# Seven block products in place of eight for the gate and up projections of a two-layer fp32 decoder

## Chip, cores and metric

The kernel runs on one core of a Trainium2 chip, as one launch. The metric is device time in microseconds (us) from start to end of the execution. Below, PE is the matrix engine (TensorE), PEld its weight loads, DVE is VectorE, ACT is ScalarE, POOL is GpSimd and SP is SyncE.

## What is computed

The input x is 512 tokens by 1024 channels in float32. Two layers run one after the other:

```python
for l in range(2):
    h = rms_norm(x, g_mix[l])
    z = h @ w_in[l]                       # 1024 x 10752
    # three mixers (retention, spatial gating, dilated attention) and gates from z
    x = x + merged @ w_o[l]
    h = rms_norm(x, g_ffn[l])
    gate, up = jnp.split(h @ w_gate_up[l], 2, axis=-1)    # 1024 x (2 x 2816)
    x = x + (jax.nn.silu(gate) * up) @ w_down[l]          # 2816 x 1024
```

The change concerns the line with gate and up. All arithmetic is float32 with float32 results.

## The kernel before

**Tiles and slabs.** Activations are held transposed: channels in partitions, the 512 tokens along the row. A layer is a list of tiles (`tiles_of_layer`, line 58). A tile is one output of 128 channels by 512 tokens, made in one PSUM bank from 4, 8 or 11 blocks of 128 x 128 weights. The feed forward is made in two halves of `FF_HALF` = 11 pairs: for each pair a tile `fgate` and a tile `fup` of 8 blocks, then 8 `down` tiles of 11 blocks that add the half to x. Tiles alternate between two main banks, so a tile can start once the tile two before it has been evacuated (`main`, in the tensor block).

**Three matmuls a block.** Full float32 precision is made from the faster float32r format. Every weight and every input is held as a high and a low part, and a block is three matmuls into the same bank: high x high, high x low, low x high (line 663). The moving operand is stored in two halves and read by turns from one and the other (`in_turn`).

**The way of a weight.** Eight blocks of 128 x 128 make a slab of 512 KB. SP loads slabs (line 551) into three raw slots; ACT copies a slab to its high part (`split`, line 829) once the slab three before it has been used; DVE subtracts to get the low part (line 994), which also frees the raw slot for SP's next load.

**The way of an output.** DVE evacuates a tile. A gate tile is multiplied by `norm_rstd` (line 1077), as h_high and h_low hold x times the gain only, and ACT applies silu (line 886). An up tile is multiplied by `norm_rstd` (line 1106) and by the gate (line 1107); ACT makes the high part (line 940) and DVE the low part (line 1128) of the product for the down tiles. A down tile is added onto x (line 1099).

**Order.** `schedule()` writes one list of steps by hand: for every tile its matmuls (`main`), the splits of the slab three ahead, what goes before the evacuation (`pre`), the evacuation (`evac`) and what follows (`post`). Each engine walks this list and does its own part in that order; semaphores tie them together. So every engine's queue is strict: a step that waits holds up all that stands behind it. SP runs a loop over slabs of its own, in which it also loads tables, and writes and reads back a small table of softmax maxima and sums per head (lines 590 to 600), which DVE needs at line 1198 (step `weigh`). GpSimd does nothing.

## Time and profile before

| | |
|---|---|
| median of 3 runs | 1954.92 us (1954.76 to 1955.07) |
| the profiled execution | 1955.0 us |
| its span, first to last instruction | 1953.2 us |
| PE busy | 1934.8 us, 99% |
| PE weight loads busy | 1690.0 us, 87% |
| DVE busy | 1135.9 us, 58% |
| ACT busy | 776.7 us, 40% |
| moved by DMA | 191.67 MB, 98 GB/s |

Busy time is the sum of the spans in which an engine had an instruction in work. Matmuls are pipelined: one is listed with its whole latency, and the next starts before it ends, so the busy time of PE says that it never stood still, and the distance between the starts says how fast it went. The granted clock of PE was 1.0 of full speed over the span. Section 5 of the page groups instructions by line and form; its last columns are the idle time just ahead of them and who ended it.

### The profile page before, as it was taken

How to read it: one execution, taken by the hardware profiler on the slowest of the kernel's cores; microseconds unless marked ns; L12 is line 12 of the kernel's file. 1: busy time of each engine (PE TensorE's matmuls, PEld its weight loads, DVE VectorE, ACT ScalarE, POOL GpSimd, SP SyncE). 2: the span in 40 equal slices, each digit the busy share in tenths (PEclk: the TensorE clock that was granted, in tenths of full speed). 3: DMA queues.
4: the chain of work that ended last, by engine and by line, in shares of the span. 5: the costliest groups of instructions: out<-in, count | busy, mean ns of one | idle time of the engine just before them, and what ended most of it. 6: DMA issues, size and time to landing. Idle time of an engine off the chain costs nothing. (4 is left out here: it accounts for less than half of the span.)

```text
span 1953.2 us, 23528 instructions
## 1 busy us (share of the span) xinstructions
PE 1934.8 (99%) x9368; PEld 1690.0 (87%) x9368; DVE 1135.9 (58%) x1523; ACT 776.7 (40%) x1090; POOL 0.2 (0%) x4
## 2 busy tenths in 40 slices
PE   7999999999999999999999999999999999999999
PEld 6888888888888888888888888888888888888888
DVE  6666667746666554355476666676366664534545
ACT  5544444533334432233345444344343343322334
POOL 0000000000000000000000000000000000000000
PEclk9999999999999999999999999999999999999999
DMA  5222222233233233333232222222223332333333
GB/s 193 87 77 76 87 82 81 92 98 98 96 120 107 97 99 98 106 107 99 97 98 92 66 79 84 82 88 94 100 97 107 109 108 97 97 97 108 98 103 123
DMA packets 65436, 191.67 MB, mean 98 GB/s; under 512 B 17200, under 2 KB 17456, under 8 KB 65328
## 3 DMA queue, kind: packets, MB, share of 16 engines
q1 hardware_dynamic: 65328, 190.17, 30.2%
q8 instruction: 75, 1.23, 0.3%
q14 instruction: 33, 0.27, 0.0%
HBM read 187.98 MB, written 2.16 MB: 97 GB/s over the span
## 5 line engine op out<-in xcount | busy, mean ns | idle before, releaser
L663 PE MATMUL bank<-h_high,w_high 128*128 128x512 f32 x2048 | 787.9, 385 | 12.3 <-DVE h_low L999 10.7
L663 PE MATMUL bank<-h_high,w_low 128*128 128x512 f32 x2048 | 777.0, 379 | 0.0
L663 PE MATMUL bank<-h_low,w_high 128*128 128x512 f32 x2048 | 776.9, 379 | 0.0
L829 ACT ACTIVATE w_high<-raw 128x1024 fp32r<-128x1024 f32 x342 | 360.9, 1056 | 951.8 <-PE bank L663 941.1
L994 DVE TENSOR_TENSOR w_low<-raw,w_high 128x1024 fp32r<-128x1024 f32 x342 | 417.1, 1222 | 91.3 <-ACT w_high L829 77.7
L663 PEld LDWEIGHTS bank<-h_high,w_high 128*128 128x128 f32 x2048 | 387.8, 189 | 70.4 <-issue 8.3
L663 PEld LDWEIGHTS bank<-h_high,w_low 128*128 128x128 f32 x2048 | 387.5, 189 | 55.1
L663 PEld LDWEIGHTS bank<-h_low,w_high 128*128 128x128 f32 x2048 | 387.9, 189 | 53.6
L663 PE MATMUL bank<-in_high,w_high 128*128 128x512 f32 x672 | 254.9, 379 | 0.0
L663 PE MATMUL bank<-in_low,w_high 128*128 128x512 f32 x672 | 254.7, 379 | 0.0
L663 PE MATMUL bank<-in_high,w_low 128*128 128x512 f32 x672 | 254.7, 379 | 0.0
L1077 DVE TENSOR_TENSOR scaled<-bank,norm_rstd 128x512 f32<-128x512 f32 x164 | 118.7, 724 | 172.9 <-PE bank L663 172.2
L663 PEld LDWEIGHTS bank<-in_high,w_high 128*128 128x128 f32 x672 | 127.0, 189 | 18.2 <-DVE in_low L1128 0.4
L663 PEld LDWEIGHTS bank<-in_high,w_low 128*128 128x128 f32 x672 | 127.0, 189 | 18.1
L663 PEld LDWEIGHTS bank<-in_low,w_high 128*128 128x128 f32 x672 | 127.0, 189 | 17.9
L1099 DVE TENSOR_TENSOR xT<-bank,xT 128x512 f32<-128x512 f32 x48 | 33.2, 692 | 147.7 <-PE bank L663 147.7
L1106 DVE TENSOR_TENSOR tmp<-bank,norm_rstd 128x512 f32<-128x512 f32 x44 | 30.4, 692 | 119.3 <-PE bank L663 117.8
L940 ACT ACTIVATE in_high<-prod 128x512 fp32r<-128x512 f32 x76 | 67.9, 894 | 78.6 <-DVEq L1096 27.5
L663 PE MATMUL bank<-work 128*128 128x128 f32 (+2 forms) x496 | 78.3, 305 | 0.0
L1128 DVE TENSOR_TENSOR in_low<-prod,in_high 128x512 fp32r<-128x512 f32 x76 | 63.4, 834 | 23.5 <-ACT in_high L940 23.5
L663 PEld LDWEIGHTS bank<-work 128*128 128x128 f32 x496 | 65.9, 191 | 6.2 <-issue 3.8
L886 ACT ACTIVATE work<-scaled 128x512 f32<-128x512 f32 x108 | 67.0, 620 | 6.4 <-DVE scaled L1077 6.2
(106 smaller groups left out, 1070.4 us busy)
## 6 DMA issues: line engine op xcount, KB each, us to landing
raw<-weights SPq DMA_DIRECT2D x343, 512.0 KB, 3.5
row<-rows SPq DMA_DIRECT2D x3, 768.0 KB, 4.5
xT<-x_t SPq DMA_DIRECT2D x8, 256.0 KB, 5.7
decay_sb<-decay SPq DMA_DIRECT2D x8, 256.0 KB, 3.8
out_t<-xT SPq DMA_DIRECT2D x8, 256.0 KB, 6.5
sgw<-spatial SPq DMA_DIRECT2D x3, 256.0 KB, 2.6
rot<-rotation SPq DMA_DIRECT2D x1, 512.0 KB, 7.8
pairs_by_token<-pairs SPq DMA_DIRECT2D x16, 4.0 KB, 4.9
```

Of the source, the lines that this page charges most:

```text
L663: return pe.matmul(o, w, m, start=start, stop=stop)
L829: act.activation(w_high[:, PART_SLOT[s], :, :], raw[:, s % RAW_SLOTS, :, :], ACT.Copy).then_inc(part_high_w.sem, 1)
L886: act.activation(dst, src, func).then_inc(activated.sem, 1)
L940: act.activation(halves(parts(key)[0]), parted(src), ACT.Copy).then_inc(high_ready.sem, 1)
L994: dve.tensor_tensor(w_low[:, PART_SLOT[s], :, :], raw[:, s % RAW_SLOTS, :, :], w_high[:, PART_SLOT[s], :, :], ALU.subtract).then_inc(part_ ...
L1077: dve.tensor_tensor(*operands, ALU.mult).then_inc(tile_stored.sem, 1)
L1099: dve.tensor_tensor(xT[:, t[-1], :], src, xT[:, t[-1], :], ALU.add).then_inc(tile_stored.sem, 1)
L1106: chain(dve.tensor_tensor(tmp[:, :], src, norm_rstd[:, :], ALU.mult))
L1128: dve.tensor_tensor(halves(lo), parted(src), halves(hi), ALU.subtract).then_inc(low_ready.sem, 1)
```

## The change

Of the 44 gate and up tiles of a layer, 8 stay as they are (`PLAIN_PAIRS` = 2, that is 4 gate and 4 up tiles). The other 36 are made in 9 units. A unit is two gate tiles and two up tiles. The inner dimension of 1024 is cut in two, and so are the 512 tokens, and the outputs are the gate and the up part: a 2 x 2 by 2 x 2 block product, A times B. It is made with seven products of quarters in place of eight (`QUICK`). Each product is 4 blocks of the inner dimension by 2 blocks of output channels by 256 tokens, three matmuls each: 24 matmuls of 256 columns. Two of the products are accumulated onto the bank of another (`ONTO`); the rest of the sums of results are made on DVE from banks and kept copies, three banks are copied or activated by ACT (`BY_SCALAR`).

The products need sums of quarters of the input (s1 to s4) and of the weights (t1 to t4). For the input, DVE first makes `normed`, x times gain times `norm_rstd` with the tokens reordered, then the sums, and ACT and DVE split the seven inputs in high and low parts, all among the steps of the eight plain tiles. The sums of weights are made in HBM before they are needed: GpSimd issues, for each unit, four plain copies and four adding transfers of 512 KB each from HBM to HBM, in six steps with a wait after each, and SP waits for them ahead of its load of a slab of sums. The down tiles are now in parts of 12 and 10 blocks; the results of a unit, f1 and f2 (each two channels tiles by 256 tokens), are stored side by side, so that the down tiles read them by turns. The load of `sgw` and `row` for the next layer moves from the first projection of branch 1 to the second down part, since the memory of `row` now also holds an input part.

```diff
+FF_BLOCKS = (12, 10)
+PLAIN_PAIRS = 2
+PAIRS = D_FF // P // 2
+QUICK_UNITS = range(PLAIN_PAIRS, PAIRS)
...
     for half in range(2):
-        for j in range(FF_HALF):
-            t += [("fgate", half, j), ("fup", half, j)]
+        if half == 0:
+            for j in range(2 * PLAIN_PAIRS):
+                t += [("fgate", 0, j), ("fup", 0, j)]
+        for u in QUICK_UNITS:
+            if (2 * u >= FF_BLOCKS[0]) == (half == 1):
+                t += [("quick", u, step) for step in range(7)]
         t += [("down", half, n) for n in range(KT)]
...
+QUICK = (("a11", "b11"), ("s2", "t2"), ("a12", "b21"), ("s1", "t1"), ("s3", "t3"), ("s4", "b22"), ("a22", "t4"))
+A11B11, S2T2, A12B21, S1T1, S3T3, S4B22, A22T4 = range(7)
+ONTO = {A12B21: A11B11, S4B22: S1T1}
+BY_SCALAR = (A11B11, A12B21, S1T1)
+SUMS = ("t1", "t2", "t3", "t4")
...
-    for half in range(2):
-        for j in range(FF_HALF):
-            post[AT["fup", half, j]] += [("high", "f", half, j), ("low", "f", half, j)]
-
+    for j in range(2 * PLAIN_PAIRS):
+        post[AT["fup", 0, j]] += [("high", "f", 0, j), ("low", "f", 0, j)]
+    for u in QUICK_UNITS:
+        post[AT["quick", u, S4B22]] += [("high", "f1", u), ("low", "f1", u)]
+        post[AT["quick", u, A22T4]] += [("second", u), ("high", "f2", u), ("low", "f2", u)]
+    post[AT["fup", 0, 0]] += [("normed", n) for n in range(4)]
+    post[AT["fgate", 0, 1]] += [("normed", n) for n in range(4, KT)]
+    post[AT["fup", 0, 1]] += [("part_high", "a11"), ("part_low", "a11"), ("input_sum", "s1")]
+    post[AT["fgate", 0, 2]] += [("input_sum", "s2"), ("part_high", "s2"), ("part_low", "s2")]
+    post[AT["fup", 0, 2]] += [("part_high", "s1"), ("part_low", "s1"), ("input_sum", "s3")]
+    post[AT["fgate", 0, 3]] += [("part_high", "s3"), ("part_low", "s3"), ("input_sum", "s4"), ("part_high", "s4"),
+                                ("part_low", "s4")]
+    post[AT["fup", 0, 3]] = [("part_high", "a12"), ("part_low", "a12")] + post[AT["fup", 0, 3]]
+    post[AT["quick", PLAIN_PAIRS, A11B11]] += [("part_high", "a22"), ("part_low", "a22")]
...
+        @block.gpsimd
+        def _(pool):
+            started = [0]
+
+            def sum_weights(dst, src, add):
+                if add:
+                    pool.dma_start(dst, src, accum_op=ALU.add, max_dma_last_dim=8 * P * 4).then_inc(weights_summed, 16)
+                else:
+                    pool.dma_start(dst, src).then_inc(weights_summed, 16)
+                started[0] += 1
+
+            for layer in range(DEPTH):
+                for n, u in enumerate(QUICK_UNITS):
+                    first = AT["quick", u, 0]
+                    b11, b21, b22 = (weights[layer * HOST_ROWS + SOURCE[BLOCKS[first + step][0][0]]]
+                                     for step in (A11B11, A12B21, S4B22))
+                    b12 = weights[layer * HOST_ROWS + B12_ROW[u]]
+                    t1, t2, t3, t4 = (sums_dram[layer, n, w] for w in range(4))
+                    sum_weights(t1, b11, False)
+                    sum_weights(t3, b22, False)
+                    pool.wait_ge(weights_summed, 16 * started[0])
+                    sum_weights(t1, b12, True)
+                    sum_weights(t3, b12, True)
+                    pool.wait_ge(weights_summed, 16 * started[0])
+                    sum_weights(t2, t1, False)
+                    pool.wait_ge(weights_summed, 16 * started[0])
+                    sum_weights(t2, b22, True)
+                    pool.wait_ge(weights_summed, 16 * started[0])
+                    sum_weights(t4, t2, False)
+                    pool.wait_ge(weights_summed, 16 * started[0])
+                    sum_weights(t4, b21, True)
+                    pool.wait_ge(weights_summed, 16 * started[0])
...
+            def load(layer, s):
+                slot, source = s % RAW_SLOTS, SOURCE[s]
+                if isinstance(source, tuple):
+                    n = source[0] - PLAIN_PAIRS
+                    sp.wait_ge(weights_summed, 16 * 8 * (layer * len(QUICK_UNITS) + n + 1))
+                    source = sums_dram[layer, n, SUMS.index(source[1])]
+                else:
+                    source = weights[layer * HOST_ROWS + source]
+                sp.dma_start(raw[:, slot, :, :].rearrange("p a n -> p (a n)"), source).then_inc(
...
-                    if s == behind(("proj", 1, 0)):
-
-                        sp.wait_ge(score_taken.sem, score_taken.at(base, "mix", HEADS - 1))
+                    if s == behind(("down", 1, 0)):
+
+                        sp.wait_ge(tile_done.sem, tile_done.at(base, AT["quick", PAIRS - 1, A22T4]))
...
+            def quick(base, i, o):
+
+                _, u, step = TILES[i]
+                slot = PART_SLOT[BLOCKS[i][0][0]]
+                high, low = input_parts(QUICK[step][0])
+                if u == PLAIN_PAIRS:
+                    pe.wait_ge(part_low.sem, part_low.at(base, QUICK[step][0]))
+                pe.wait_ge(part_low_w.sem, part_low_w.at(base, BLOCKS[i][0][0]))
+                for k in range(4):
+                    hi, lo = in_turn(high[:, k, :]), in_turn(low[:, k, :])
+                    for c in range(2):
+                        part = o[:, c * 2 * P:(c + 1) * 2 * P]
+                        wh, wl = w_high[:, slot, 2 * k + c, :], w_low[:, slot, 2 * k + c, :]
+                        onto = step in ONTO
+                        pe.matmul(part, wh, hi, start=k + c == 0 and not onto, stop=False, skip_group_check=onto)
+                        pe.matmul(part, wh, lo, start=False, stop=False, skip_group_check=onto)
+                        last = pe.matmul(part, wl, hi, start=False, stop=k == 3 and c == 1, skip_group_check=onto)
+                last.then_inc(tile_done.sem, 1)
...
+                            if t[2] in BY_SCALAR:
+                                act.wait_ge(tile_done.sem, tile_done.at(base, i))
+                            if t[2] == A11B11:
+                                if t[1] > PLAIN_PAIRS:
+                                    act.wait_ge(tile_stored.sem, tile_stored.at(base, AT["quick", t[1] - 1, S2T2]))
+                                act.activation(kept_first, bank_of(base, i)[:, :], ACT.Copy).then_inc(bank_copied.sem, 1)
+                            elif t[2] == A12B21:
+                                if t[1] > PLAIN_PAIRS:
+                                    act.wait_ge(product.sem, product.at(base, "f1", t[1] - 1))
+                                else:
+                                    act.wait_ge(product.sem, product.at(base, "f", 0, 2 * PLAIN_PAIRS - 1))
+                                act.activation(first_gate, bank_of(base, i)[:, :], ACT.Silu).then_inc(bank_copied.sem, 1)
+                            elif t[2] == S1T1:
+                                if t[1] > PLAIN_PAIRS:
+                                    act.wait_ge(product.sem, product.at(base, "f2", t[1] - 1))
+                                act.activation(kept_s1t1, bank_of(base, i)[:, :], ACT.Copy).then_inc(bank_copied.sem, 1)
+                            elif t[2] == A22T4:
+                                act.wait_ge(tile_stored.sem, tile_stored.at(base, i))
+                                act.activation(sum3, sum3, ACT.Silu).then_inc(second_gate.sem, 1)
...
+                            first = i - t[2]
+                            if t[2] == S2T2:
+                                dve.wait_ge(bank_copied.sem, bank_copied.at(base, first + A11B11))
+                                dve.tensor_tensor(sum2, src, kept_first, ALU.add).then_inc(tile_stored.sem, 1)
+                            elif t[2] == S3T3:
+                                dve.wait_ge(tile_stored.sem, tile_stored.at(base, first + S2T2))
+                                dve.tensor_tensor(sum3, src, sum2, ALU.add).then_inc(tile_stored.sem, 1)
+                                dve.wait_ge(bank_copied.sem, bank_copied.at(base, first + S1T1))
+                                dve.wait_ge(tile_stored.sem, tile_stored.at(base, i))
+                                chain(dve.tensor_tensor(kept_s1t1, kept_s1t1, sum3, ALU.subtract))
+                            elif t[2] == S4B22:
+                                tmp_free()
+                                dve.tensor_tensor(tmp[:, :], src, sum2, ALU.subtract).then_inc(tile_stored.sem, 1)
+                                dve.wait_ge(tile_stored.sem, tile_stored.at(base, i))
+                                dve.wait_ge(bank_copied.sem, bank_copied.at(base, first + A12B21))
+                                dst = product_slot(("f1", t[1]))
+                                tmp_read.append((product, ("f1", t[1])))
+                                dve.tensor_tensor(dst, first_gate, tmp[:, :], ALU.mult).then_inc(product.sem, 1)
+                            else:
+                                dve.tensor_tensor(sum3, src, sum3, ALU.add).then_inc(tile_stored.sem, 1)
...
+                    elif kind == "second":
+                        u, = key
+                        dve.wait_ge(second_gate.sem, second_gate.at(base, u))
+                        dst = product_slot(("f2", u))
+                        dve.tensor_tensor(dst, sum3, kept_s1t1, ALU.mult).then_inc(product.sem, 1)
+                    elif kind == "normed":
+                        n, = key
+                        dve.scalar_tensor_tensor(normed[:, n, :, :], xT[:, n, :].rearrange("p (q m) -> p m q", m=4),
+                                                 vec[:, n:n + 1], norm_rstd[:, :].rearrange("p (q m) -> p m q", m=4),
+                                                 ALU.mult, ALU.mult).then_inc(normed_ready.sem, 1)
```

The lines left out hold the same pattern: the sums of the input and their parts, the signals, the layout of the weights on the host, and the placement of the new buffers over old ones that rest in the feed forward.

## Rows read from the trace of the kernel before

**Rows 1.** Page: busy time, share of the span, instructions; slices of PE and clock.

```profile
PE 1934.8 (99%) x9368; PEld 1690.0 (87%) x9368; DVE 1135.9 (58%) x1523; ACT 776.7 (40%) x1090; POOL 0.2 (0%) x4
...
PE   7999999999999999999999999999999999999999
...
PEclk9999999999999999999999999999999999999999
```

**Rows 2.** PE timeline, plain tile: start us, us, engine, line, operation, count.

```profile
660.87 0.38 PE L663 MATMUL bank<-h_high,w_high 128*128 128x512 f32 x1
661.09 0.38 PE L663 MATMUL bank<-h_low,w_high 128*128 128x512 f32 x1
```

**Rows 3.** Waits of PE: who waited for whom, us in total, times, longest.

```profile
PE bank L663 <- DVE h_low L999: 10.7, 4, 8.3
PE bank L749 <- ACT work L969: 1.6, 2, 0.8
```

**Rows 4.** DVE timeline, first pairs of the feed forward, layer 0; idle before in brackets.

```profile
655.89 0.69 DVE L1077 TENSOR_TENSOR scaled<-bank,norm_rstd 128x512 f32<-128x512 f32 x1 [1.14 <-PE bank L663]
657.04 1.23 DVE L994 TENSOR_TENSOR w_low<-raw,w_high 128x1024 fp32r<-128x1024 f32 x1 [0.46 <-ACT w_high L829]
661.07 0.69 DVE L1106 TENSOR_TENSOR tmp<-bank,norm_rstd 128x512 f32<-128x512 f32 x1 [2.81 <-PE bank L663]
661.80 0.69 DVE L1107 TENSOR_TENSOR prod<-tmp,work 128x512 f32<-128x512 f32 x1
662.73 1.23 DVE L994 TENSOR_TENSOR w_low<-raw,w_high 128x1024 fp32r<-128x1024 f32 x1 [0.24 <-DVE prod L1107]
...
666.25 0.69 DVE L1077 TENSOR_TENSOR scaled<-bank,norm_rstd 128x512 f32<-128x512 f32 x1 [1.54 <-PE bank L663]
...
672.15 0.69 DVE L1107 TENSOR_TENSOR prod<-tmp,work 128x512 f32<-128x512 f32 x1
...
682.51 0.69 DVE L1107 TENSOR_TENSOR prod<-tmp,work 128x512 f32<-128x512 f32 x1
```

**Rows 5.** PE timeline around a burst of short matmuls.

```profile
62.34 1.68 PE L663 MATMUL bank<-work 128*128 128x128 f32 x8
63.86 0.60 PE L749 MATMUL bank<-identity,scaled 128*128 128x128 f32 x4
```

**Rows 6.** Weight loads (PEld) of the same stretch.

```profile
64.19 0.19 PEld L663 LDWEIGHTS bank<-h_high,w_high 128*128 128x128 f32 x1
64.30 0.19 PEld L663 LDWEIGHTS bank<-h_low,w_high 128*128 128x128 f32 x1
```

**Rows 7.** PE timeline, four matmuls of one column.

```profile
645.82 0.58 PE L663 MATMUL bank<-ones,work 128*128 128x1 f32 x4
```

**Rows 8.** Groups by form, PE: busy us, mean ns; straight and alternating operands.

```profile
L663 PE MATMUL bank<-in_high,w_high 128*128 128x512 f32 x672 | 254.9, 379 | 0.0
...
L663 PE MATMUL bank<-in_high,ones_r 128*128 128x512 f32 x32 | 13.5, 422 | 0.3 <-DVE in_low L1145 0.3
L663 PE MATMUL bank<-in_low,ones_r 128*128 128x512 f32 x32 | 12.6, 394 | 0.0
```

**Rows 9.** Line 1080, plain and permuted evacuations: ns min/median/max.

```profile
L1080 DVE TENSOR_TENSOR work<-bank,norm_rstd x48: 684/1058/1097, 26.3 to 1200.3; 128x512 f32<-128x512 f32 x48
```

**Rows 10.** ACT timeline beside rows 4, and two ACT groups by form.

```profile
655.95 1.06 ACT L829 ACTIVATE w_high<-raw 128x1024 fp32r<-128x1024 f32 x1 [2.45 <-PE bank L663]
656.91 0.62 ACT L886 ACTIVATE work<-scaled 128x512 f32<-128x512 f32 x1
...
L905 ACT ACTIVATE in_high<-work 128x512 fp32r<-128x512 f32 x32 | 19.7, 615 | 0.0
...
L976 ACT ACTIVATE work<-bank 128x512 f32<-128x512 f32 x8 | 4.8, 597 | 12.4 <-PE bank L663 12.4
```

**Rows 11.** PE timeline at the start.

```profile
8.88 0.63 PE L663 MATMUL bank<-h_low,w_high 128*128 128x512 f32 x1
9.30 0.63 PE L663 MATMUL bank<-h_high,w_low 128*128 128x512 f32 x1
...
12.64 0.38 PE L663 MATMUL bank<-h_low,w_high 128*128 128x512 f32 x1
12.85 0.38 PE L663 MATMUL bank<-h_high,w_low 128*128 128x512 f32 x1
...
16.79 0.48 PE L663 MATMUL bank<-h_high,w_high 128*128 128x512 f32 x1 [1.63 <-DVE h_low L999]
```

**Rows 12.** DMA issues: KB each, median us from issue to landing.

```profile
raw<-weights SPq DMA_DIRECT2D x343, 512.0 KB, 3.5
...
out_t<-xT SPq DMA_DIRECT2D x8, 256.0 KB, 6.5
```

**Rows 13.** Windows: busy us and count by engine, clock, DMA share, GB/s.

```profile
core 0: us, PE busy (x) PEld busy (x) DVE busy (x) ACT busy (x) POOL busy (x), PEclk, DMA share, GB/s
0.00:10.00 10.00, 1.68 (x4) 1.44 (x5) 4.12 (x9) 6.05 (x9) 0.20 (x4) 1.00 0.77 243
10.00:20.00 10.00, 7.61 (x27) 5.44 (x27) 9.68 (x14) 8.14 (x13) 0.00 (x0) 1.00 0.85 308
...
660.00:680.00 20.00, 20.00 (x94) 17.52 (x93) 10.55 (x12) 7.07 (x8) 0.00 (x0) 1.00 0.29 98
```

**Rows 14.** SP timeline: the exchange of the first head's pairs.

```profile
77.58 0.38 SPq L590 DMA_DIRECT2D pairs_by_token<-pairs  x1
...
82.87 0.32 SPq L598 DMA_DIRECT2D pairs<-pairs_by_token  x1
```

**Rows 15.** DVE timeline behind that exchange; idle before line 1198.

```profile
82.71 1.09 DVE L1080 TENSOR_TENSOR work<-bank,norm_rstd 128x512 f32<-128x512 f32 x1 [2.16 <-PE bank L663]
...
85.69 0.16 DVE L1198 TENSOR_TENSOR shift<-pairs 128x8 f32<-128x8 f32 x1
...
92.27 1.07 DVE L1080 TENSOR_TENSOR work<-bank,norm_rstd 128x512 f32<-128x512 f32 x1
...
  DMA pairs<-pairs_by_token: 2.4, 3
```

174 lines of the change are left out of this document (148 added, 26 removed).

## Prediction

> **What bounds the kernel now.** I read the page's busy shares first: PE is busy 99% of 1953.2 us, DVE 58%, ACT 40%, POOL nothing, and the slices show a PE that never rests after the first [rows 1]. PE's busy time does not tell its rate, because matmuls overlap, so I went to the PE timeline: matmuls of 512 columns start every 0.216 us although each is listed with 0.38 us [rows 2]. 512 columns at the upper clock level, 2.4 GHz, are 0.2133 us, so the stream of columns is the limit. The longest group of waits of PE is 10.7 us, 8.3 of it before the first matmul, the next 1.6 us [rows 3]. The end is therefore set by the number of columns times 1/2.4 GHz, and what every other engine does costs nothing as long as PE finds its weights, its inputs and a free bank.
>
> The feed forward has 44 tiles a layer of 8 blocks x 3 matmuls. A gate and its up tile take 10.36 us (the second product of a pair recurs at 661.80, 672.15 and 682.51) [rows 4], so two pairs, what one unit of the change replaces, take 20.72 us.
>
> **Term 1, the seven products.** A unit becomes 7 steps of 24 matmuls of 256 columns, each with its own weight load: 168 loads where there were 96. The columns are 7/8 of those before. Half of 0.2133 is 0.1067, and with the 2 to 3 ns by which a matmul exceeds its columns now it is 0.109 us. The question is whether a weight load fits in that. It is listed with 189 ns, but that is latency: after a short burst two loads for h_high and h_low start at 64.19 and 64.30, 0.11 us apart; the four transposes before them take 0.60 us of which the last is 0.27, so they start 0.11 apart with one load each; eight records of full-precision matmuls, some of them 256 wide in two passes, need (1.68 - 0.38)/7 = 0.186 us [rows 5, 6]. No stretch shows more than a few short matmuls in a row, so sustained issue is not shown. I take 0.110 us: 2.64 us a step, 18.48 us a unit. At the edges 0.109 gives 18.31 us and 0.112 (four loads with matmuls of a single column take 0.58 us, the last of it 0.24, so even with no columns to stream they are (0.58 - 0.24)/3 = 0.113 apart) 18.8 us [rows 7]. A matmul whose moving operand is read straight through costs more than one read with alternating halves (422 and 394 ns against 379) [rows 8]; the new ones alternate too, but at half the distance, which no row shows. That is a rival below.
>
> **Term 2, can DVE and ACT feed it.** A slab of weights is now used up in 2.64 us instead of 5.18. Durations: the high part on ACT 1.06 us, the low part on DVE 1.23 us (1.15 to the next start), a 512 column DVE operation 0.69, an ACT one 0.60 to 0.62, a product's high part on ACT unstrided 0.62 (the two outputs f1 and f2 are stored contiguously) [rows 4, 9, 10]. Per unit DVE has 7 x 1.15 + 7 x 0.69 + 2 x 0.69 = 14.3 us, ACT 7 x 1.0 + 3 x 0.6 + 0.62 + 2 x 0.62 = 10.7 us, both under 18.5. But the work is uneven. I followed the two queues, with t = 0 at the first step and a tile finished 0.2 us after the next begins. Step S4B22 is done at 16.0: DVE subtracts and multiplies (17.5), makes a low part (18.7) and the low part of f1 (19.3). Step A22T4, done at 18.7, therefore gets its addition at 19.3 to 20.0; ACT's silu ends at 20.6; DVE makes a low part meanwhile (21.1), multiplies (21.8); ACT converts f2's high part to 22.4. Only then does ACT, whose queue is strict, take the next unit's weights (23.4) and copy A11B11 out of its bank (23.95). A12B21 adds onto that bank and may start at 24.0; PE is there at 18.48 + 5.28 = 23.76. So 0.2 us a unit is lost, and a slower PE would lose less. A unit takes 18.7 us, saves 20.72 - 18.66 = 2.06, and 18 units save **37.1 us**. Bounds: 18.31 without a stall saves 43.4, 18.82 saves 34.2.
>
> **Term 3, the inputs.** In the eight plain tiles ahead of the first unit DVE gets 8 normed tiles, 4 sums, 7 low parts; ACT gets 7 high parts. A normed tile reads two operands with a step of four; the nearest row is a permuted evacuation at 1.06 us against 0.69 plain [rows 9]; the bounds are 0.75 (the plain form) and 1.5. Sums and low parts are 1024 wide, 1.15 each. Together 8 x 1.0 + 11 x 1.15 = 20.7 us. In the rows before, DVE idles 1.54 + 0.46 + 2.81 + 0.24 = 5.05 us in each pair of tiles [rows 4], about 15 us between the first up tile's end and the last's, and now also waits for ACT's high parts. Followed: normed 0 to 3 end at 658.9 and delay the evacuation due at 655.9 by 3 us; the next four end near 664.9; the up tile due at 661.1 is stored at 666.3, which holds PE for 0.3 to 0.5 us; the next up tile costs 0.6; the last gate tile is evacuated at 682.7 and s3, s4 end at 688.4, so the last up tile, finished at 683, is stored at 689.9. The unit's second step needs its bank at 685.4: 4.6 us lost, then 1.1 more until DVE has caught up. 6.8 us a layer, **+13.6 us** (bounds 2 x 3 and 2 x 10). If the normed tiles are cheap, this is where I am too high.
>
> PE at rest for 4.6 us may come back at the lower clock. At the start the first matmuls are 0.43 us apart, the 1.2 GHz level, and 0.216 from 12.6 us on, after some 4 us of work; the stalls of up to 1.6 us that followed did not bring it back [rows 11]. The Trainium skill (TensorE: Matmul & The Clock Gate, What you observe) says the same of the start, and that an idle engine falls back; by it each entry would cost some 2 us more. No row shows a fall in mid-kernel, and the sum is without it.
>
> **Term 4, the adding transfers.** GpSimd starts them at time zero and nothing throttles it: per unit six steps in a chain, two of them double, 144 transfers of 512 KB. A load of 512 KB lands after 3.5 us, a store of 256 KB after 6.5 [rows 12]. Six steps of 3.5 are 21 us a unit, eight of 6.5 are 52. I take 40, as stores and read-and-add cost more than loads: 720 us for 18 units. Units 0 to 8 are there by 360 us, first wanted at 690, so the sums are never late (that needs over 100 us a unit). They collide instead.
> - Start: the DMA engines are 77% and 85% busy in the first two 10 us [rows 13]. ACT works through x without a pause from 5.2 us on. One to three megabytes more in that time: **+3 us** (0 to 6).
> - The exchange of pairs: written at 77.58, read back from 82.87, used at 85.69; over the run DVE waits 2.4 us for it, so it has no slack [rows 14, 15]. A tile ended at 82.71, the next two by 93.1; the bank that PE wants then is evacuated from 92.27 to 93.34, behind the exchange in DVE's queue. Each of two hops may sit behind transfers of 512 KB; four heads of layer 0 fall in this time; 1.5 us each gives **+6 us** (0 to 20).
> - Slab loads have over 10 us of slack in tiles of 5.18 us. In the units a raw slot goes round in 3.5 + 1.06 + 1.23 + some 1.2 of queueing and handing over = 7.0 us against 3 x 2.64 = 7.92: slack 0.9 us. With the chain ended at 720 us only the first unit or two of layer 0 meet it: **+3 us** (0 to 10).
>
> The Trainium skill (DMA: Bandwidth & Descriptors, Anatomy of one DMA) gives 2.0 us plus bytes at 436 GB/s for a transfer that GpSimd issues; an estimate from it is 3.2 us a transfer and about 22 us a unit, so that the last would end near 400 us and the 3 us of slab loads would be nil. It is for copies without adding and no run here shows it.
>
> **Small ones.** The two down stages keep their 176 blocks a layer; the last f2 is ready some 5.5 us after the last step, wanted after 8 or 10 blocks (5.2 or 6.5 us): +1 us in all. The load of sgw and row moves past SP's down slab and waits for a tile that is about to end; SP's next slab waits behind it, and is wanted 10 us later: nothing. The wait on the sums stands ahead of SP's loads, with nothing else queued but them, and the sums are long there.
>
> **Sum.** The profiled execution took 1955.0 us (span 1953.2), the median is 1954.92, so no correction. 1955.0 - 37.1 + 13.6 + 3 + 6 + 3 + 1 = **1944.5 us**.
>
> **Rivals.**
> - *Short matmuls are slower than half.* If the alternating read at half the distance, or the issue of a load and a matmul every 0.11 us, limits, take the excess of the straight read: 394/379 to 422/379 on 0.110 is up to 0.12 us. At 0.119 a unit takes 20.0, the units save 13 us, and the costs of 26.6 stand: 1968 us. At 0.125 it is 1987. For: no row has such a stream. Against: loads and transposes 0.11 apart. 0.12.
> - *The adding transfers run into the units.* This ends on the slow side. If a unit of sums takes 52 us or more, the chain lasts beyond 920 us and loads of slabs and sums share the engines through all nine units of layer 0. From a landing of 4.4 us the slot's round exceeds 7.92 us. At 5.25 us each of 63 slabs is 0.3 us late (17 us), at 7 us 0.86 (54 us). Middle 35: 1944.5 - 3 + 35 = 1976 us. For: 199 GB/s of slabs alone against the 308 GB/s at 85% busy at the start. 0.16.
> - *The costs cancel the gain.* Normed tiles at 1.5 us and pairs at 3 us a head: +8 and +6, 1951 to 1959. 0.12.
> - *The costs are hidden.* Entry 3 us a layer, no collision: 1955 - 40 + 7 = 1922, between 1918 and 1930. 0.10.
> - *The change doesn't do what it says:* the trace would show 96 matmuls of 512 columns a unit; the lists of tiles leave no room for it, under 0.01.
> - Forecast, 1930 to 1951: 0.50.
>
> About 0.2% is what a measurement of this kernel can tell from no change, 3.9 us. Faster 0.60, same 0.12, slower 0.28. The range holds the forecast, the hidden case from 1922 on, the cancelling one and the slow rivals up to 1982.
>
> **What the trace would show.** Term 1: starts of 256 column matmuls 0.110 us apart within a step. Term 2: a small idle of PE before the third step of a unit, released by an ACT copy. Term 3: PE idle of 4 to 5 us at the second step of the first unit, waiting for the evacuation of the last plain tile. Term 4: GpSimd's last transfer near 720 us; later PE idles in layer 0's heads than in layer 1's. The prediction is wrong if the step is longer than 2.7 us, if a slab's landing in the units exceeds 4.4 us, or if the chain of sums outlasts 900 us.

## The result, and the profile after

| | before | after |
|---|---|---|
| median, four runs each | 1954.98 us | 1963.89 us (1962.86 to 1965.45) |
| ratio | | 1.0045 [1.0034, 1.0057] |
| span of the profiled execution | 1953.2 us | 1961.6 us |

The change makes the kernel 0.45% slower. I had expected it 0.5% faster, at 1944.5 us. The time lies inside the range, but my likeliest case had the wrong sign. It lies in a gap between my rivals: above the one in which the costs cancel the gain (1951 to 1959), and below the one of slow short matmuls (1968).

The page of the kernel after. Rows on queues give packets, MB and share of the 16 DMA engines; rows on DMA issues KB each and us to landing. They answer to [rows 1, 12].

```profile
PE 1917.3 (98%) x10664; PEld 1712.7 (87%) x10664; DVE 1249.1 (64%) x1633; ACT 855.1 (44%) x1194; POOL 97.1 (5%) x148
...
q1 hardware_dynamic: 73104, 218.49, 35.9%
q0 software_dynamic: 12672, 75.51, 17.1%
...
raw<-weights SPq DMA_DIRECT2D x325, 512.0 KB, 3.8
weight_sums<-weights POOLq DMA_DIRECT2D x108, 512.0 KB, 5.9
...
weight_sums<-weight_sums POOLq DMA_DIRECT2D x36, 512.0 KB, 4.2
```

PE still is the engine that sets the time (98% busy), but it now stands still where it did not before. Its waits in the kernel after (us in total, times, longest), to be held against [rows 3]:

```profile
PE bank L816 <- DVE h_low L1209: 12.8, 5, 10.2
PE bank L942 <- DVE work L1483: 9.3, 3, 3.6
PE bank L834 <- DVEq L1343: 7.1, 2, 3.6
PE bank L816 <- DVEq L1343: 5.4, 2, 2.7
```

Apart from the start, the large waits are of two kinds: L942 lies in the attention heads of layer 0, the two on L1343 in the entry to the units, once a layer each. `DVEq L1343` is the signal with which DVE reports an up tile as stored, and its bank as free. One wait of 2.8 us (L908, at 30 us) still belongs to the start.

**Where the time went.** The first matmul of each stage on the PE timeline splits the span. First the feed forward of layer 0 in the kernel before: first half's pairs, its down tiles, second half's pairs, down tiles.

```profile
638.09 0.38 PE L663 MATMUL bank<-h_high,w_high 128*128 128x512 f32 x1
...
754.11 0.38 PE L663 MATMUL bank<-in_high,w_high 128*128 128x512 f32 x1
...
811.09 0.38 PE L663 MATMUL bank<-h_high,w_high 128*128 128x512 f32 x1
...
925.05 0.38 PE L663 MATMUL bank<-in_high,w_high 128*128 128x512 f32 x1
```

The second half's 22 tiles take 113.96 us, 5.18 each; the first half's take 116.02, since the norm's short matmuls and small gaps stand among the first tiles, some 2.1 us. So the eight tiles that stay plain took 8 x 5.18 + 2.1 = 43.5 us.

The same in the kernel after: plain tiles, four units, down tiles, five units, down tiles; then the plain tiles and the four units of layer 1.

```profile
658.72 0.38 PE L816 MATMUL bank<-h_high,w_high 128*128 128x512 f32 x1
...
707.37 0.27 PE L834 MATMUL bank<-a_high,w_high 128*128 128x256 f32 x1
707.47 0.28 PE L835 MATMUL bank<-a_low,w_high 128*128 128x256 f32 x1
707.59 0.28 PE L836 MATMUL bank<-a_high,w_low 128*128 128x256 f32 x1
...
788.11 0.38 PE L816 MATMUL bank<-in_high,w_high 128*128 128x512 f32 x1
...
850.28 0.27 PE L834 MATMUL bank<-a_high,w_high 128*128 128x256 f32 x1
...
944.38 0.38 PE L816 MATMUL bank<-in_high,w_high 128*128 128x512 f32 x1
...
1619.98 0.38 PE L816 MATMUL bank<-h_high,w_high 128*128 128x512 f32 x1
...
1668.85 0.27 PE L834 MATMUL bank<-a_high,w_high 128*128 128x256 f32 x1
...
1749.50 0.38 PE L816 MATMUL bank<-in_high,w_high 128*128 128x512 f32 x1
```

- **Units.** Five units take 944.38 - 850.28 = 94.10 us, 18.82 each, which is 168 matmuls 0.112 us apart and no idle time. Against 20.72 they save 1.90 a unit, 34.2 us for 18.
- **Entry.** The plain tiles take 48.65 us in layer 0 and 48.87 in layer 1 (+5.2 and +5.4), the four units behind them 80.74 and 80.65 where 4 x 18.82 = 75.3 would do (+5.5 and +5.4). Together +21.5 us.
- **Layer 0 before its feed forward.** It begins at 658.72 in place of 638.09: +20.6 us. Layer 1's projections, mixers and output take the same 623.33 us in both (982.50 to 1605.83 before, 996.65 to 1619.98 after).
- 21.5 + 20.6 - 34.2 = +7.9; the spans differ by 8.4.

**The entry, in rows.** DVE timeline and then PE timeline of the kernel after, just ahead of the first unit of layer 0; idle before in brackets.

```profile
675.28 6.15 DVE L1351 SCALAR_TENSOR_TENSOR normed<-xT,vec,norm_rstd 128x512 f32<-128x512 f32 x4
...
683.05 5.63 DVE L1351 SCALAR_TENSOR_TENSOR normed<-xT,vec,norm_rstd 128x512 f32<-128x512 f32 x4
688.58 0.70 DVE L1340 TENSOR_TENSOR tmp<-bank,norm_rstd 128x512 f32<-128x512 f32 x1
```

```profile
690.22 0.79 PE L816 MATMUL bank<-h_high,w_high 128*128 128x512 f32 x1 [2.69 <-DVEq L1343]
690.80 0.63 PE L816 MATMUL bank<-h_low,w_high 128*128 128x512 f32 x1
...
693.34 0.38 PE L816 MATMUL bank<-h_low,w_high 128*128 128x512 f32 x1
...
709.93 0.28 PE L836 MATMUL bank<-a_high,w_low 128*128 128x256 f32 x1
713.84 0.58 PE L834 MATMUL bank<-s_high,w_high 128*128 128x256 f32 x1 [3.63 <-DVEq L1343]
714.21 0.42 PE L835 MATMUL bank<-s_low,w_high 128*128 128x256 f32 x1
...
716.99 0.38 PE L836 MATMUL bank<-s_high,w_low 128*128 128x256 f32 x1
```

Four normed tiles take 5.6 to 6.15 us, 1.5 each, and stand in DVE's queue ahead of an up tile's evacuation (688.58), so PE waits 2.69 us for a bank. Then it works at 0.43 us a matmul, the 1.2 GHz level (granted clock 0.50 from 690.20 to 693.30), and loses 1.5 us more. At the second product of the unit it waits 3.63 us and runs 256 columns 0.215 apart until 716.99, which loses another 1.6. 2.7 + 1.5 + 3.6 + 1.6 = 9.4 of the 10.7 us; the rest is waits of under 0.5 us.

**The exchange of pairs, in rows.** In an exchange, the softmax table of a head is written to HBM and read back in another layout. The first head of layer 0, on SP, GpSimd, DVE and PE of the kernel after, as [rows 14, 15] for the kernel before.

```profile
89.97 0.32 SPq L751 DMA_DIRECT2D pairs<-pairs_by_token  x1
```

```profile
85.39 1.69 POOL L667 DMA_DIRECT2D weight_sums<-weights  x2 [4.43 <-DMA weight_sums<-weights]
99.70 0.52 POOL L669 DMA_DIRECT2D weight_sums<-weight_sums  x1 [12.62 <-DMA weight_sums<-weights]
```

```profile
99.77 0.17 DVE L1466 TENSOR_TENSOR shift<-pairs 128x8 f32<-128x8 f32 x1 [7.34 <-DMA pairs<-pairs_by_token]
```

```profile
103.76 1.75 PE L942 MATMUL bank<-identity,work 128*128 128x128 f32 x7 [3.61 <-DVE work L1483]
105.17 0.78 PE L816 MATMUL bank<-h_high,w_high 128*128 128x512 f32 x1
105.73 0.63 PE L816 MATMUL bank<-h_low,w_high 128*128 128x512 f32 x1
```

Before, the table was read from 82.87 and used at 85.69. Now it is read from 89.97 and used at 99.77, 70 ns after the two adding transfers issued at 85.39 have landed. DVE waits 7.34 us, PE 3.61, and then PE's granted clock is 0.50 until 109.58 (matmuls of 512 columns 0.43 apart), some 2.9 us lost on top. Over the run the waits of DVE are these, against 2.4 us in 3 before [rows 15]; 20.6 us of them fall on the four heads of layer 0:

```profile
DVE shift L1466 <- DMA pairs<-pairs_by_token: 24.9, 8, 7.3
```

The four exchanges do not cost the same. From the moment SP issues a head's write to the same moment of the next head (of the last head, to the feed forward), the kernel after falls back by 6.7, 5.2, 0.0 and 2.2 us.

The packet records of the two traces show what the read waits for. The 512 packets of 8 bytes of the first head's read start 1.4 us after the issue and within 0.7 us of each other before (84.31 to 85.00), but 5.8 us after the issue and spread over 3.6 us after (95.74 to 99.31). Their landing follows the last of them by 0.3 and 0.4 us. So the packets themselves start late. From 87 to 90 us no packet at all starts on SP's queue, though a slab load was issued at 86.25, while some 50 packets of the adding transfers do.

**The clock, in rows.** Windows of one stretch of the heads before, then of the same stretch and of the entry in layer 0 after; the columns are as in [rows 13].

```profile
75.00:140.00 65.00, 65.00 (x352) 57.97 (x351) 42.59 (x72) 34.03 (x71) 0.00 (x0) 1.00 0.28 82
```

```profile
75.00:140.00 65.00, 61.39 (x320) 54.24 (x319) 39.60 (x68) 27.77 (x53) 8.09 (x12) 0.95 0.71 178
650.00:730.00 80.00, 73.04 (x400) 64.76 (x399) 62.91 (x66) 36.71 (x44) 8.04 (x12) 0.96 0.69 185
```

Between 10 and 1950 us the granted clock never leaves 1.00 in the kernel before. In the kernel after it stands at 0.50 for 31 us in all: 7 in the start (around 22 and 33 us), 10 at the first two heads, 7 in each entry. PE worked in 29 of these 31 us, and half of that, 14.6 us, is lost: 3.4 in the start, 4.6 at the heads, 6.6 in the entries. These are parts of the costs above, not costs beside them.

### The profile page after: what moved, and what is told of

It reads as the page before. It is cut to its first block and busy times, and to the rows that moved or that the text cites. A ratio compares the mean times of both kernels' runs of the same rounds, so it can differ in the third digit from the quotient of the medians.

```text
span 1961.6 us, 26697 instructions
## 1 busy us (share of the span) xinstructions
PE 1917.3 (98%) x10664; PEld 1712.7 (87%) x10664; DVE 1249.1 (64%) x1633; ACT 855.1 (44%) x1194; POOL 97.1 (5%) x148
## 5 line engine op out<-in xcount | busy, mean ns | idle before, releaser
L816 PE MATMUL bank<-h_high,w_high 128*128 128x512 f32 x1472 | 574.4, 390 | 20.2 <-DVE h_low L1209 12.8
L816 PE MATMUL bank<-h_low,w_high 128*128 128x512 f32 x1472 | 562.6, 382 | 0.0
L816 PE MATMUL bank<-h_high,w_low 128*128 128x512 f32 x1472 | 562.5, 382 | 0.0
L816 PEld LDWEIGHTS bank<-h_high,w_low 128*128 128x128 f32 x1472 | 281.0, 191 | 40.7
L834 PE MATMUL bank<-s_high,w_high 128*128 128x256 f32 x576 | 160.0, 278 | 7.1 <-DVEq L1343 7.1
L835 PE MATMUL bank<-s_low,w_high 128*128 128x256 f32 x576 | 159.9, 278 | 0.0
L836 PE MATMUL bank<-s_high,w_low 128*128 128x256 f32 x576 | 159.8, 277 | 0.0
L834 PEld LDWEIGHTS bank<-s_high,w_high 128*128 128x128 f32 x576 | 111.9, 194 | 7.5 <-DVEq L1343 7.5
L836 PEld LDWEIGHTS bank<-s_high,w_low 128*128 128x128 f32 x576 | 112.0, 194 | 0.0
L835 PEld LDWEIGHTS bank<-s_low,w_high 128*128 128x128 f32 x576 | 111.9, 194 | 0.0
```

What stands on the lines that cost most here:

```text
L816: return pe.matmul(o, w, m, start=start, stop=stop)
L834: pe.matmul(part, wh, hi, start=k + c == 0 and not onto, stop=False, skip_group_check=onto)
L835: pe.matmul(part, wh, lo, start=False, stop=False, skip_group_check=onto)
L836: last = pe.matmul(part, wl, hi, start=False, stop=k == 3 and c == 1, skip_group_check=onto)
```

## The experiments

The theory after reading the two traces: the units do what they should; the adding transfers cost 20.6 us, all before the first feed forward, at the start and at the exchanges; the entry costs 21.5 us, through slow normed tiles, through the place of the later input sums, and through the clock. The rivals: the transfers cost nothing and the stretch is longer for another reason (moved buffers); the loss is one of bandwidth in all stages; the adding costs, and plain copies would not. What the transfers cost ahead of the first feed forward is read, in each profiled execution, from the start of its first matmul: 638.09 before, 658.72 after.

### The sums left out, and the sums alone

SP loads a slab of the given weights where it waited for a sum:

```diff
-                    sp.wait_ge(weights_summed, 16 * 8 * (layer * len(QUICK_UNITS) + n + 1))
-                    source = sums_dram[layer, n, SUMS.index(source[1])]
+                    source = weights[layer * HOST_ROWS + B12_ROW[source[0]]]
...
-        @block.gpsimd
```

> The changed kernel without any of GpSimd's 144 transfers; SP loads an untouched slab of the same size in place of each slab of sums, so the units compute with other weights than the sums. All else is as changed. Theory: in layer 0 the transfers cost what lies between the two traces before the feed forward, 658.7 - 638.1 = 20.6 us, and nothing later, since both layers' feed forwards take the same 337.9 us. Expected 1963.9 - 20.6 = 1943.3 us. Rival: the transfers also slow the eight plain tiles and the first units of layer 0, then below 1940. Rival: most of the 20.6 us comes from the changed program itself (more instructions, other buffers), then above 1955.

Measured: 1943.94 us, ratio 0.9936 [0.9916, 0.9956] (one of its four executions took 4070 us and is left out of the ratio). The feed forward begins here, on PE's timeline:

```profile
637.72 0.38 PE L780 MATMUL bank<-h_high,w_high 128*128 128x512 f32 x1
```

So the whole 20.6 us is the transfers; the moved buffers cost nothing. What is left is a gain of 11 us from the seven products with their entry. That it is near the 10.4 us of my whole forecast is chance: for these parts alone I had 37.1 - 13.6 - 1 = 22.5.

The other way round, the kernel before with GpSimd's block added (same count and sizes, sources among its own slabs; nobody reads the sums):

```diff
+        @block.gpsimd
...
+                for n in range(9):
...
+                    first = layer * SLABS + BLOCKS[AT["fgate", 0, 0]][0][0] + 4 * (n % 5)
+                    b11, b21, b22, b12 = (weights[first + step] for step in range(4))
```

> The kernel before, with only GpSimd's chain of copies and adding transfers put in (same number, sizes and waits; nobody uses the sums). Theory: the 20.6 us of layer 0 come with the transfers alone: 1955.0 + 20.6 = 1975.6 us. Rival: they need the change's other parts, then near 1955; or they also harm the feed forward where the old slab rate leaves 10 us of slack, then above 1980.

Measured: 1971.27 us (1968.20 to 1980.02), ratio 1.0090 [1.0066, 1.0115]; the feed forward begins at 653.28, 15.2 us late, and nothing is lost after it. The transfers alone cost 15 us in the profiled execution, 16 in the median, against 20.6 expected. The two runs add up roughly: 0.9936 x 1.0090 = 1.0025 against 1.0045, within what these runs vary.

### Exchanges or start

The exchange is left out; DVE takes the head's own values, so the two token halves' shares are wrong:

```diff
-                        write_pairs(base, swap_at[s])
-                        read_pairs(base, swap_at[s - 1])
...
-                        dve.wait_ge(pairs_swapped, 32 * (base // STRIDE * HEADS + h + 1))
```

> The changed kernel without the exchange of pairs through HBM (eight times two writes and two reads); DVE uses the core's own values in place of the swapped ones, so the attention weights are not the reference's. GpSimd's transfers stay. Theory: of the 20.6 us about 6.6 are lost by 34 us from the start (first loads) and 14 at the exchanges, where DVE waits 7.3, 6.8 and 6.5 us and PE stands still and comes back at the lower clock level: 1963.9 - 14 = 1950 us. Rival: slab loads or DVE itself are slowed by GpSimd's descriptors: stays at 1962 to 1965.

Measured: 1951.37 us, 0.9983 [0.9974, 0.9992]. The feed forward begins at 645.74, 7.65 us late, and that whole lag is there early: one of DVE's low parts of a slab stands at 41.37 us where it stood at 33.72. After that the transfers cost nothing for 600 us although they go on until some 708. So start 7.7 us, exchanges 20.6 - 7.7 = 12.9 us, bandwidth in all stages nothing. The split is good to 1 us: in the kernel after itself the same low part stands at 40.38, which makes the start 6.7 and the exchanges 14.0. The start can be seen on ACT's timeline, first two rows of before and then one of after, where ACT waits for x:

```profile
5.20 1.06 ACT L829 ACTIVATE w_high<-raw 128x1024 fp32r<-128x1024 f32 x1 [2.97 <-DMA raw<-weights]
6.16 0.74 ACT L834 ACTIVATE h_high<-xT,first_gain 128x512 fp32r<-128x512 f32 x1
```

```profile
8.43 0.75 ACT L1009 ACTIVATE h_high<-xT,first_gain 128x512 fp32r<-128x512 f32 x1 [2.29 <-DMA xT<-x_t]
```

### Adding or moving

```diff
-                    pool.dma_start(dst, src, accum_op=ALU.add, max_dma_last_dim=8 * P * 4).then_inc(weights_summed, 16)
+                    pool.dma_start(dst, src).then_inc(weights_summed, 16)
```

> The changed kernel with the 72 adding transfers made plain copies of the same size in the same chain, so the sums are wrong. Theory: what an exchange waits behind is the pair of adding transfers (85.4 to 99.7 us in the trace), which read two streams; with copies the step is near 6 us and the exchanges lose about half: 1955 to 1959 us, and the chain ends near 500 us in place of 712. Rival: copies are as bad as adding ones, as only the number of queued bytes counts: 1962 to 1965 us, chain end near 700.

Measured: 1954.22 us (1949.23 to 1960.14), 0.9998 [0.9988, 1.0007]; the feed forward begins at 646.04, 8.0 us late. GpSimd's last issue is at 577 us (708.6 with adding). The same bytes go in 4608 packets in place of 12672. The wait of DVE for pairs is still 16.9 us in 6, but PE's wait at the heads falls from 9.3 to 3.1 us, and the granted clock stays at 1.00 there. So in the profiled executions adding makes 12.6 of the 20.6 us and moving the rest; by the medians adding makes 9.7 us; the exchanges collide with plain copies too, only for less long. I had the chain's end at 500: a plain copy from HBM to HBM, 4.8 us (4.0 for the copies out of sums), is not as quick as a load, 3.6.

### The sums in another place

GpSimd begins each layer's sums only after its last exchange:

```diff
             for layer in range(DEPTH):
+                pool.wait_ge(pairs_swapped, 32 * HEADS * (layer + 1))
                 for n, u in enumerate(QUICK_UNITS):
```

> The changed kernel, complete, but GpSimd starts each layer's nine units of sums only after the fourth exchange of pairs of that layer has landed. Theory: the sums then run from about 270 to 625 us and from 1240 to 1600 us, where slab loads have slack and nothing is exchanged, and the whole 20.6 us come back: 1943 to 1945 us, as with the transfers left out (1943.9). Rival: the transfers also cost elsewhere (the retention phase, the spatial tables, the first units if a unit of sums takes over 40 us): 1948 us or more.

Measured: 1944.79 us (1944.30 to 1945.71), 0.9945 [0.9928, 0.9962]. The feed forward begins at 638.02. The chain runs from 267 to some 620 us; a window of GpSimd's busy stretch (columns as [rows 13]) has as much traffic as before and PE at 1.00:

```profile
480.00:620.00 140.00, 140.00 (x666) 122.92 (x665) 85.56 (x103) 51.89 (x62) 18.75 (x28) 1.00 0.76 203
```

The same transfers at the same 76% of the DMA engines cost nothing here. It is the place that costs, not the amount: what they must not stand beside is a small transfer that has no slack, and the first loads. The entries alone got dearer, 12.0 us a layer in place of 10.7: the second wait is 4.65 us instead of 3.6, and PE then works at the 0.50 clock for 5.8 us where it did so twice for 3.1 to 3.4. With this one line the change makes the kernel 10 us faster than before, where it was 9 slower.

Two weaker cures, on the kernel after. The first starts the chain once x is in:

```diff
+            pool.wait_ge(low_ready.sem, low_ready.at(0, "h", 0, KT - 1))
```

> The changed kernel, GpSimd's chain held back only until x has been split (18 us). With the exchanges left out (e3) a lag of 7.7 us was left in layer 0, and the two traces show 6.7 of it by 34 us from the start. Theory: that part belongs to the first loads, which share the DMA engines with the first transfers: 1963.9 - 5 = 1959 us or less; the third slab's load at 18 us may still meet the chain, which would leave 1 or 2 us. Rival: the 7.7 us are spread over slab loads later on: 1963 or more.

Measured: 1961.59 us (1956.08 to 1968.36), 1.0038 [1.0021, 1.0054], so the median moved by 2.3 us and not by 7.7. In its profiled execution, the fastest of the five at 1956.08, the start is free (lag 0.2 us at 93 us), but the exchanges cost 12.2 us (feed forward at 650.50). The expectation held for the start and failed for the total: what the exchanges cost is not a constant. That a chain which begins later meets them in other phases is the likely reason, not a shown one.

The second waits after every transfer, so that no two adding transfers are under way together:

```diff
                     sum_weights(t1, b11, False)
+                    pool.wait_ge(weights_summed, 16 * started[0])
```

> The changed kernel with a wait after every transfer: eight steps a unit in place of six, never two transfers in flight. Theory: an exchange waits for what is queued when it arrives, so with one transfer in flight it waits 3 to 5 us where it waited 7 (two adding transfers took 14 us together beside the exchange); about half of the 13 us of the exchanges comes back: 1955 to 1959 us, and the chain ends later than 712. Rival: the wait depends on adding as such and on the many 8 byte pieces of the exchange, not on how much is queued: 1962 to 1965 us.

Measured: 1958.82 us (1952.11 to 1964.30), 1.0016 [1.0003, 1.0028]. Its profiled execution is one of the slower ones, 1962.48. There the feed forward begins at 646.60, 8.5 us late in place of 20.6; DVE's wait for pairs is still 18.5 us in 7. But the chain now ends at 861 us and reaches into the units: the first four take 90.0 us in place of 80.7, and PE waits there 4.1 us in 2 for a copy by ACT (line 1049), whose strict queue also holds the splits of late slabs: ACT waits 14.6 us in 5 for slabs of sums there, and 1.4 us in 1 in the kernel after. That is the rival "the adding transfers run into the units" in small: 9 us for a chain that lasts 150 us longer.

### The entry

The permutation on the write, so that both operands of the normed tile are read in order:

```diff
-                        dve.scalar_tensor_tensor(normed[:, n, :, :], xT[:, n, :].rearrange("p (q m) -> p m q", m=4),
-                                                 vec[:, n:n + 1], norm_rstd[:, :].rearrange("p (q m) -> p m q", m=4),
+                        dve.scalar_tensor_tensor(normed[:, n, :, :].rearrange("p m q -> p q m"),
+                                                 xT[:, n, :].rearrange("p (q m) -> p q m", m=4),
+                                                 vec[:, n:n + 1], norm_rstd[:, :].rearrange("p (q m) -> p q m", m=4),
```

> The changed kernel with one difference: the eight normed tiles a layer read x and norm_rstd straight and write with a step, where they read with a step of four and wrote straight. In the trace four took 6.15 us, 1.5 each; a permuted evacuation writes with a step and takes 1.06. Theory: 8 x 0.45 = 3.6 us a layer off DVE's queue, and the idle of 2.7 us at the second up tile with the stretch at the lower clock behind it (2 us or so) goes: 4 to 6 us a layer, 1952 to 1956 us. Rival: the cost is in the step on either side, or the second stall takes what the first gives back: 1961 to 1964 us.

Its expectation was written for the kernel after with this edit alone. The kernel that ran also had the late start of the sums, so it is to be held against that run. Measured: 1936.36 us (1935.71 to 1937.39), 0.9903 [0.9889, 0.9918], 8.4 us less than 1944.79. Groups by form of the two kernels, late sums first:

```profile
L1352 DVE SCALAR_TENSOR_TENSOR normed<-xT,vec,norm_rstd 128x512 f32<-128x512 f32 x16 | 23.6, 1553 | 0.0
```

```profile
L1352 DVE SCALAR_TENSOR_TENSOR normed<-xT,vec,norm_rstd 128x512 f32<-128x512 f32 x16 | 15.9, 1119 | 0.0
```

7.7 us less on DVE in all, 3.9 a layer, and the 2.7 us wait at the up tile is gone. The plain tiles are back to 43.9 us; the wait ahead of the second product stays at 4.6 us a layer, and the entry costs 7.4 us in layer 0 and 7.9 in layer 1 in place of 12.0. Then the same edit on the kernel after alone, as it was meant:

> The changed kernel with only the normed tiles permuted on write, and GpSimd's chain from the start on, as in the change (the run e6_permute_on_write also had the late start of e5, against what its expectation says; beside e5 it was 8.4 us faster). Theory: the two effects add: 1963.9 - 8.4 = 1955.5 us. Rival: the chain meets the entry of layer 0, and the gain there is another: over 1958 or under 1953.

Measured: 1955.19 us (1951.12 to 1969.51), 1.0010 [0.9992, 1.0029]: 8.7 us less than 1963.89. As far as a kernel can tell that varies by 18 us from run to run, the two causes add.

Next, with late sums and the write permutation, the work that stands ahead of the last up tile's evacuation moves behind it, to the first and second product of the unit:

```diff
-    post[AT["fgate", 0, 3]] += [("part_high", "s3"), ("part_low", "s3"), ("input_sum", "s4"), ("part_high", "s4"),
-                                ("part_low", "s4")]
+    post[AT["fgate", 0, 3]] += [("part_high", "s3"), ("part_low", "s3")]
...
+    post[AT["quick", PLAIN_PAIRS, A11B11]] += [("input_sum", "s4"), ("part_high", "s4"), ("part_low", "s4")]
+    post[AT["quick", PLAIN_PAIRS, S2T2]] += [("part_high", "a22"), ("part_low", "a22")]
```

> Complete kernel: sums later as in e5, permuted on write as in e6, and in the order of steps the sum s4 with its parts moves behind the first product of the first unit and a22's parts behind the second, since they are wanted at the sixth and seventh. Theory: entry costs 10.9 us a layer as changed; 4 to 6 go with the cheaper normed tiles and about 3.5 of the stall before the second product with the move: 1944 - 2 x 8 = 1928 us (1925 to 1933). Rival: DVE's backlog only moves into the first unit, and the gain over e5 and e6 together is nothing: 1935 us or more.

Measured: 1932.41 us (1931.31 to 1933.94), 0.9883 [0.9868, 0.9898]. The 4.6 us became 1.2, but a new wait of 2.7 us a layer came ahead of the fourth product, behind the s4 work (5.4 us in all, for DVE line 1282). This wait is 2.71 us in either layer, and the clock fell after it in one of them only:

```profile
694.00:697.50 3.50, 3.49 (x18) 3.49 (x19) 3.36 (x3) 1.42 (x2) 0.00 (x0) 0.57 0.36 95
...
1650.80:1654.30 3.50, 3.48 (x31) 3.48 (x32) 3.37 (x3) 1.87 (x4) 0.00 (x0) 1.00 0.38 88
```

The three products behind the wait take 9.56 us in layer 0 and 8.14 in layer 1, and the four units 81.10 and 79.66, so the fall by itself costs 1.4 us. Next, the same work one product later each:

```diff
+    post[AT["quick", PLAIN_PAIRS, S2T2]] += [("input_sum", "s4"), ("part_high", "s4"), ("part_low", "s4")]
+    post[AT["quick", PLAIN_PAIRS, A12B21]] += [("part_high", "a22"), ("part_low", "a22")]
```

> Complete kernel, as e8_later_and_spread, but s4 and its parts come behind the second product of the first unit and a22's parts behind the third, each one step later. In e8's trace PE idles 2.7 us before the fourth product of the first unit, since DVE has s4's sum and low part (689.8 to 693.3) ahead of the evacuation that frees the bank. Theory: that idle goes, 2 x 2.7 us: 1932.4 - 5 = 1927 us. Rival: the sixth product now waits for s4, and the time stays within 1 us of e8.

Measured: **1928.46 us (1927.86 to 1928.82), ratio 0.9862 [0.9847, 0.9877]**, faster than both kernels. Its waits of PE in the entry, with the granted clock at 1.0 over the span:

```profile
PE bank L835 <- ACT work L1054: 2.6, 2, 1.3
PE bank L835 <- DVEq L1344: 2.3, 2, 1.2
```

The entry costs 3.4 us a layer here (plain tiles 43.85 us, four units 78.3), in place of 12.0 with late sums alone.

### The straight read

With late sums, the products read their moving operand straight through (the tokens of a tile then come in another order):

```diff
-hi, lo = in_turn(high[:, k, :]), in_turn(low[:, k, :])
+hi, lo = high[:, k, :], low[:, k, :]
```

> As e5_sums_later, but the 256 column matmuls read their moving operand straight instead of by turns from its two halves, so the tokens of the units come out in another order. Measures the cadence alone. If weight loads set the 0.112 us between starts and reading by turns is free, it stays at 0.112 us (1944 us). If reading straight costs per column as it does for the 512 wide ones (235 ns between starts where 216 is usual), 0.118 to 0.120 us and 18 x 168 x 0.007 = 21 us more: 1965 us.

Measured, in a single execution: 1965.73 us beside 1945.71 of the profiled one with late sums, spans 1963.9 and 1943.9. PE timeline of a unit:

```profile
687.15 0.28 PE L836 MATMUL bank<-a_low,w_high 128*128 128x256 f32 x1
687.27 0.28 PE L837 MATMUL bank<-a_high,w_low 128*128 128x256 f32 x1
```

0.120 us apart in place of 0.112. 0.008 x 168 x 18 = 24 us, 20 measured. So the alternating read at half the distance does its work: the rival "short matmuls are slower than half" named a true price (0.119 to 0.12 us), but of the other read.

## Why the prediction was wrong

Every mechanism that cost time was named in the prediction, but three terms were too small, and the fall of the clock was left out of the sum ("the sum is without it"), though it is in all three. The three largest misses (entry 7.9, exchanges 6.9, start 4.7) are all to the bad side and make 19.5 us, the units add 2.9, and 3.5 came back from the last two terms: 18.9 us net, against a forecast gain of 10.4.

| term | forecast | measured | by |
|---|---|---|---|
| units | -37.1 | -34.2 | 0.112 us in place of 0.110 |
| entry, two layers | +13.6 | +21.5 | plain tiles and four units; normed tiles, clock |
| transfers at the start | +3 | +7.7 | the exchange left out (6.7 in the kernel after's own rows) |
| transfers at the exchanges | +6 | +12.9 | the same, against the kernel after (14.0 by its own rows) |
| transfers in the units | +3 | 0 | five units without idle time |
| small ones | +1 | 0.5 | remainder |

The measured column adds up to +8.4 us on the span, where I had -10.5.

- **Term 1.** I chose 0.110 between 0.109 and 0.112, and gave the upper edge from one-column matmuls 0.113 apart [rows 7]. That row had the right number. Matmuls of one column and of 256, each with a load, are 0.113 and 0.112 us apart, which suggests that the pair of load and matmul sets the pace and not the columns; no run here shows it. 168 matmuls x 0.002 x 18 = 6 us, of which 3 come back, since Term 2's stall of 0.2 us a unit never came: by my own words a slower PE loses less.
- **Term 2.** The idle before a unit's third step isn't there in the steady units. DVE and ACT can feed the products.
- **Term 3, a step that failed.** I took 1.0 us for a normed tile, from the permuted evacuation at 1.06 [rows 9], which writes with a step; here two operands are read with a step of four and the tile takes 1.55. 16 x 0.5 = 8 us of DVE's time, and PE pays it because DVE's queue is strict: with the write permuted, 1.12 us a tile, 8.4 us came back. The wait that I named, 4.6 us at the unit's second product, is there to the tenth in the runs with late sums; in the kernel after it is 3.6, and the 2.7 at the up tile, where I had 0.3 to 0.5, is the new part. So my walk through the queues named the right waits, and the price of the tile in it was wrong.
- **The clock, the term put at nothing.** I had priced the fall to the lower level at 2 us an entry and left it out, as no row showed one in mid-kernel, and of the start and the exchanges I did not ask it. Now the rows show it at all three, 14.6 us of lost PE time, of which 3.3 us an entry. The net loss is smaller: after the fall at the up tile the next wait is 3.6 us, and 4.65 where the clock had not fallen. No run holds the clock apart from the waits; only the two layers of one run, above, show a fall by itself, at 1.4 us. The Trainium skill (TensorE: Matmul & The Clock Gate, What's actually happening) says that a matrix engine without work goes back to the throttled state. This trace agrees, with a granted clock of 0.50 after idle times of 3.63, 3.61 and 2.69 us. With that sentence taken into the sum I would have stood 4 us higher. The length of the wait alone does not decide it. In these traces every wait of 3.07 us or more, other than the one before the first matmul, was followed by the lower clock; of the shorter ones, down to 1.5 us, some were and some were not.
- **The conditions.** Of the three points that would make the prediction wrong none occurred: a step takes 24 x 0.112 = 2.69 us, slabs land in 3.6 to 3.8 us (medians of the run; 3.6 for the slabs of sums), the chain ended before 900. Each was just met or met with room, and still the sum failed. They guarded the large rivals and not the sizes of the small terms.
- **Term 4.** The chain's end was right: last issue at 708.6 us for 720. Right too: exchanges without slack, and that only layer 0's heads pay. Wrong were the sizes. I had 1.5 us a head where the mean is 3.2 to 3.5 and the first two take 6.7 and 5.2, and nothing for the clock. For the start I had 3 us in place of 6.7 to 7.7. For the transfers I had taken one price of each hop; the rows show that a read of a few KB issued 4.6 us behind a double adding transfer of 14 us lands with it. The Trainium skill (DMA: Bandwidth & Descriptors, Queues, rings and completion order) says that each DMA engine takes turns between queues packet by packet, by which a small read would pass a large transfer early. This trace does not bear that out: the read here took 9.8 us from its issue, and its first packet started after 5.8. The same page's fit (Anatomy of one DMA) gave an estimate of 3.2 us a transfer; measured were 5.9 and 4.2.
- **Chances.** I had the costs of entry, exchanges and clock as separate terms near their low ends, and gave 0.12 to all of them coming out high together. They are not independent: one price of a normed tile moves both entries, and every wait of over 3 us also brought the lower clock. The rival with normed tiles at 1.5 us and 3 us a head, 0.12, had both its conditions met (1.55 and 3.2 to 3.5); what lifted the time above its 1959 is the start and the slower units. Of the bounds, 0.112 us and the 20 us for the exchanges held; the entries at 21.5 us lie above their 20, the start above its 6, and a normed tile just above its 1.5.

What stays open: why packets on SP's queue start late beside the adding transfers. That the packets of the read start late is shown (first head above; in the second head the first starts 2.3 us after the issue and the last after 6.9, against 1.4 and 2.2 before), and so is that their landing adds only 0.4 us. What holds them back, no run here tells. Open too is why the variants with the chain beside the exchanges vary by 11 to 18 us from run to run (4 us without the exchange, and 2.6 us in the four executions of the kernel after itself), while those with a late chain stay within 1.0 to 2.6 us. That it is the phase of the two is argued, not shown.

## What to carry to other kernels

Count a background stream not by its bandwidth but by what it runs beside: 76% busy DMA engines cost nothing over 350 us of large loads with slack, and 13 us over four small exchanges without. Price the work that prepares for a faster inner loop by its strict queue: move it behind the evacuations that the matrix engine waits for, and write permuted rather than read permuted. Where the sum makes the matrix engine wait for 3 us or more, add a fall of its clock: it lost 1.6 to 2.9 us each time here, some of which the next wait gave back.

## What the runs showed of the hardware

- float32r matmuls of 256 columns, each with its own weight load, start 0.112 us apart when the moving operand is read by turns from two halves, 0.120 when it is read straight through. 512 columns take 0.216 [rows 2].
- A DVE scalar_tensor_tensor on 128 x 512 float32 takes 1.55 us with both tensors read at a step of four, 1.12 us with one write at a step of four.
- From HBM to HBM, 512 KB issued by GpSimd: 4.2 us as a copy (36 of them); 5.9 is the median of 72 additions and 36 copies; two additions at once beside loads and a small exchange took 14 us. Packets of 8 bytes on SP's queue started 5.8 us after their issue beside them, 1.4 without them.
- PE's clock fell to the 1.2 GHz level (granted clock 0.50) in mid-kernel after each of the idle times from 3.07 to 4.65 us. After 2.71 us in one and the same kernel it fell once and once did not, and it did not after 2.61 us in the kernel after.
